# A residual stream parked in HBM during the expert stages, and its SBUF space given to two experts

## The reference, cut to what matters

```python
for layer in range(2):
    x = x + mixer[layer](rmsnorm(x, norm_mix[layer]))
    x = x + hier_moe(rmsnorm(x, norm_ffn[layer]))     # both groups share the weights
y = rmsnorm(x, norm_final)

def hier_moe(t):                       # t: (576, 1024)
    combine = ...                      # (576, 32): two nonzero weights per row
    g = einsum('td,edf->tef', t, w_gate)          # w_gate, w_up: (32, 1024, 128)
    u = einsum('td,edf->tef', t, w_up)
    hid = silu(g) * u * combine[..., None]
    return einsum('tef,efd->td', hid, w_down)     # w_down: (32, 128, 1024)
```

## Time and profile before

| | |
|---|---|
| median of three runs | 926.05 us |
| the profiled execution's own time | 925.76 us |
| its span, first to last instruction | 923.8 us |
| TensorE matmuls busy | 768.5 us, 83% |
| VectorE busy | 405.7 us, 44% |
| ScalarE busy | 259.9 us, 28% |
| GpSimd busy | 151.3 us, 16% |
| mean granted TensorE clock | 0.916 |
| DMA moved | 201.81 MB, mean 218 GB/s |
| of it on SP's queue, q1 | 161.77 MB |
| scatters and gathers, q0 | 19.75 MB |
| ScalarE's queue, q10 | 19.46 MB |

### The profile page before, as it was taken

The page is one execution under the profiler, slowest core; times in us unless marked ns, Lnnn a source line. Parts: engine busy times, 40 slices in busy tenths (PEclk is TensorE's granted clock), DMA queues, the critical chain, the costliest instruction groups (busy, mean ns, idle before and its releaser), DMA issues.

```text
span 923.8 us, 12813 instructions
## 1 busy us (share of the span) xinstructions
PE 768.5 (83%) x4895; PEld 481.0 (52%) x4895; DVE 405.7 (44%) x1001; ACT 259.9 (28%) x554; POOL 151.3 (16%) x233
## 2 busy tenths in 40 slices
PE   3899977999899898999733689799999888999730
PEld 2344445868545695555423567544345487555410
DVE  3378695867588370111128677301112162211118
ACT  6020034635111202322213355310014311322113
POOL 1020003000779001332110201000000001333110
PEclk9999996979999889999976899899999979999885
DMA  9462135000532898999869787780131296999946
GB/s 341 145 201 101 51 112 221 2 0 2 200 117 114 290 411 303 409 411 402 351 201 309 198 209 174 212 313 0 49 133 46 70 396 245 405 409 408 396 156 226
DMA packets 75381, 201.81 MB, mean 218 GB/s; under 512 B 14872, under 2 KB 29592, under 8 KB 74264
## 3 DMA queue, kind: packets, MB, share of 16 engines
q1 hardware_dynamic: 58360, 161.77, 48.7%
q0 software_dynamic: 9696, 19.75, 6.1%
q10 hardware_dynamic: 7264, 19.46, 5.8%
HBM read 171.64 MB, written 39.39 MB: 228 GB/s over the span
## 4 chain that ended last, share of the span: by engine, by line
PE 63%; DMA 11%; DVE 11%; ACT 6%; SPq 5%; issue 3%; POOL 0%; PEldq 0%; DVEq 0%; POOLq 0%; PEld 0%; ACTq 0%
PE PSUM L2049 14%; PE PSUM L1852 10%; PE PSUM L1637 8%; PE PSUM L1796 7%; PE PSUM L1873 5%; DMA RING<-in_moe_w_up 3%; PE PSUM L1840 3%; DMA RING<-in_attn_w_qkv 3%; DVE X L1515 2%; SPq L476 2%; PE PSUM L1727 2%; PE PSUM L1999 2%; PE PSUM L1995 2%; DVE XNT L773 2%; PE PSUM L1594 2%
## 5 line engine op out<-in xcount | busy, mean ns | idle before, releaser
L1637 PE MATMUL PSUM<-RING,XNT 128*128 128x512 f32 (+2 forms) x256 | 94.5, 567 | 4.3 <-DMA RING<-in_attn_w_qkv 3.6
L1852 PE MATMUL PSUM<-PH 128*64 128x256 f32 x448 | 85.6, 399 | 8.4 <-DMA PH<-in_moe_w_up 3.9
L671 POOL DMA_INDIRECT PH<-xn_scratch,PH x32 | 32.5, 1017 | 342.4 <-DVEq L1459 247.7
L2049 PE MATMUL PSUM<-PH,XNT 128*128 128x512 f32 (+1 forms) x220 | 88.1, 593 | 0.3 <-PE PSUM L2049 0.3
L1852 PE MATMUL PSUM<-RING,PH 128*64 128x256 f32 x384 | 69.4, 392 | 11.2 <-DMA PH<-in_moe_w_up 6.4
L1594 PE MATMUL PSUM<-ONES,IDENT 128*128 128x128 f32 x348 | 49.8, 314 | 24.1 <-DVEq L1518 23.9
L1490 DVE TENSOR_TENSOR PH<-PH,PSUM 128x128 f32<-128x128 f32 x32 | 9.2, 289 | 136.3 <-ACT PH L976 136.3
L1637 PEld LDWEIGHTS PSUM<-RING,XNT 128*128 128x128 f32 (+1 forms) x256 | 40.4, 177 | 53.9 <-issue 47.7
L1852 PEld LDWEIGHTS PSUM<-PH 128*64 128x64 f32 x448 | 51.6, 144 | 27.0 <-issue 11.9
L1796 PE MATMUL PSUM<-RING,PH 128*128 128x512 f32 (+1 forms) x160 | 62.6, 593 | 0.0
L1594 PEld LDWEIGHTS PSUM<-ONES,IDENT 128*128 128x128 f32 x348 | 48.8, 229 | 24.5 <-DVEq L1518 24.0
(11 more groups left out here) (378 smaller groups left out, 1366.7 us busy)
## 6 DMA issues: line engine op xcount, KB each, us to landing
PH<-in_moe_w_gate SPq DMA_DIRECT2D x28, 512.0 KB, 10.9
PH<-in_moe_w_up SPq DMA_DIRECT2D x28, 512.0 KB, 13.2
RING<-in_moe_w_gate SPq DMA_DIRECT2D x24, 512.0 KB, 11.5
RING<-in_moe_w_up SPq DMA_DIRECT2D x24, 512.0 KB, 16.0
RING<-in_moe_w_down SPq DMA_DIRECT2D x24, 512.0 KB, 16.3
PH<-in_moe_w_down SPq DMA_DIRECT2D x24, 512.0 KB, 14.8
RING<-in_attn_w_qkv SPq DMA_DIRECT2D x4, 1536.0 KB, 18.3
XNT<-in_moe_w_gate SPq DMA_DIRECT2D x12, 512.0 KB, 16.6
```

The lines of the kernel that those rows point to most:

```text
L671: pool.indirect_dma_start(out=XG[:, i % 2, :], out_offset=None, in_=xn_d[layer], in_offset=bass.IndirectOffsetOnAxis(ap=IDX[:, i:i + 1], a ...
L1637: last = te.matmul(PSUM[lo:hi, b0 + col // 512, col % 512:col % 512 + n], XT[:, c, t * P:t * P + r], RING[:, c // 2, (c % 2) * QKV + col:( ...
L1852: last = te.matmul(PSUM[m * 64:(m + 1) * 64, 2 + i % 2, 0:2 * FF], XGT[:, i % 2, c, m * 64:(m + 1) * 64], gu[:, :, c, :], start=(c == 0), ...
L2049: last = te.matmul(PSUM[p0:p0 + r, 2 * (i % 2) + w, :], XT[:, c, t * P:t * P + r], slot(SLOT[q])[:, (2 * (c % 3) + w) * 512:(2 * (c % 3) + ...
```

## The change

`X` is stored to a new HBM tensor, `residual_scratch`, tile by tile, just ahead of the store of the normed tile and on the same queue. The waits for the stores count both, 32 for a tile instead of 16. From then on two more experts use its space: expert 12 of each layer has its three matrices there, expert 13 its gate and up matrices, while its down matrix lies in `GAM`. These two places (`PARKED`) are used once in a layer. After them the twelve slots go round as before (`ring`), so each later expert stands two places later in that round. The two parked experts share one semaphore, and a wait for either waits for both. `DF` goes from 6 to 7. `residual_back` reads `X` back into place behind the last load of the layer, and the combine waits for a tile's rows and its part of `X`.

The norm's weights are now read in the middle of the stage (after pair 8's work on ScalarE), since `GAM` holds a down matrix until pair 6 is done. The read of the S5 inputs waits for pair 14 instead of pair 13, because another expert is the last in its place. At the end of the S5 layer two semaphores are merged into others (`h_transposed` into `st_transposed`, `h_copied` into `hs_in`), and `ring_wait` of TensorE takes the semaphore from the new function `filled`; these lines are not shown.

```diff
@@ -125,16 +125,24 @@
 
         xn_d = [nc.dram_tensor("xn_scratch", (NTOK, D), FP).ap()] * 2
         y_d = [nc.dram_tensor("y_scratch", (2 * NTOK, D), FP).ap()] * 2
+        x_d = nc.dram_tensor("residual_scratch", (NTOK, D), FP).ap()
         blk_d = nc.dram_tensor("block_scratch", (NB, P, BLK_F), FP).ap()
         in_d = nc.dram_tensor("input_scratch", (P, IN_F), FP).ap()
         XBASE = PH_F - XS * RW
         ZER = PH[:, PH_F - D:PH_F]
 
+        XFLAT = X.rearrange("p t d -> p (t d)")
+        PARKED = RS + XS + NS + 1
+
         def gate_up_part(k):
+            if k >= PARKED:
+                return XFLAT[:, (k - PARKED) * 2 * D:(k - PARKED + 1) * 2 * D]
             return ODD_GU if k == RS + XS + NS else slot(k)[:, 0:2 * D]
 
         def down_parts(k):
 
+            if k >= PARKED:
+                return [XFLAT[:, 4 * D:5 * D] if k == PARKED else GAM[:, :]]
             if k == RS + XS + NS:
                 return [PH[:, odd_at:odd_at + 512], MRC]
             return [slot(k)[:, 2 * D:3 * D]]
@@ -341,16 +349,29 @@
 
         Q_M = [Q_M0, Q_M1]
         ORDER0, ORDER1 = [3, 4, 5, 6, 7, 0, 1, 2, 10, 8, 9, 11], [1, 2, 3, 4, 5, 7, 6, 0, 10, 8, 9, 11]
-        SLOT = ([0, 1, 2, 3] + [0, 1, 2] + [ORDER0[e % len(ORDER0)] for e in range(NE)] 
+
+        def ring(order):
+
+            n = len(order)
+            return [order[e] if e < n else PARKED + e - n if e < n + 2 else order[(e - 2) % n] for e in range(NE)]
+
+        SLOT = ([0, 1, 2, 3] + [0, 1, 2] + ring(ORDER0) 
                 + [3, 4, 5, 7, 3, 4, 5, 7] + [3, 4, 5, 7, 6, 0]
-                + [ORDER1[e % len(ORDER1)] for e in range(NE)])
+                + ring(ORDER1))
         OV_SLOTS = [0, 1]
 
         def full(q):
 
+            if SLOT[q] >= PARKED:
+                last = q + PARKED + 1 - SLOT[q]
+                return 16 * sum(LOADS[j] for j in range(last + 1) if SLOT[j] >= PARKED)
             return 16 * sum(LOADS[j] for j in range(q + 1) if SLOT[j] == SLOT[q])
 
-        DF = 6
+        def filled(q):
+
+            return S(f"ring_full{min(SLOT[q], PARKED)}")
+
+        DF = 7
 
         def down_full(layer, i):
 
@@ -468,28 +489,35 @@
                         if e == RS + XS:
                             sp.wait_ge(S("logits"), layer + 1)
                         if e == RS + XS + 1:
-                            sp.wait_ge(S("xn_stored"), 16 * NT * (layer + 1))
+                            sp.wait_ge(S("xn_stored"), 32 * NT * (layer + 1))
                         if freed(q):
                             room(q, 0)
                         r = gate_up_part(SLOT[q])
                         for w, src in enumerate((w_gate, w_up)):
                             sp.dma_start(r[:, w * D:(w + 1) * D].rearrange("p (c f) -> p c f", c=KC),
-                                         src[layer, e].rearrange("(p c) f -> p c f", p=P)).then_inc(S(f"ring_full{SLOT[q]}"), 16)
+                                         src[layer, e].rearrange("(p c) f -> p c f", p=P)).then_inc(filled(q), 16)
                     for e in (2 * i - 2, 2 * i - 1) if i else ():
                         q = Q_M[layer] + e
                         if freed(q):
                             room(q, 1)
                         parts = down_parts(SLOT[q])
+                        if SLOT[q] > PARKED:
+                            sp.wait_ge(S("xn_done"), NT * (2 + 2 * layer))
                         if len(parts) > 1:
                             sp.wait_ge(S("routed"), layer + 1)
                         n = D // len(parts)
                         for j, dst in enumerate(parts):
                             sp.dma_start(dst, w_down[layer, e, :, j * n:(j + 1) * n]).then_inc(S(f"down_full{(i - 1) % DF}"), 16)
 
+            def residual_back(layer):
+                sp.wait_ge(S("expert_out"), PAIRS * layer + 7)
+                for t in range(NT):
+                    sp.dma_start(X[0:ROWS[t], t, :], x_d[t * P:t * P + ROWS[t], :]).then_inc(S(f"yg_full{t}"), 16)
+
             def overflow(layer):
 
                 sp.wait_ge(S("routed"), layer + 1)
-                sp.wait_ge(S("xn_stored"), 16 * NT * (layer + 1))
+                sp.wait_ge(S("xn_stored"), 32 * NT * (layer + 1))
                 sp.wait_ge(S("overflow_known"), layer + 1)
                 n = sp.value_load(OVR[0:1, layer, 0:1], min_val=0, max_val=OVP)
                 before = sp.value_load(OVR[0:1, 0, 0:1], min_val=0, max_val=OVP) if layer else 0
@@ -522,7 +550,8 @@
                 ring_load(Q_SSM + k, [(slot(SLOT[Q_SSM + k])[:, 0:BLK_F], blk_d[k])])
 
             experts(0)
-            sp.wait_ge(S("ring_free"), Q_M0 + 28)
+            residual_back(0)
+            sp.wait_ge(S("ring_free"), Q_M0 + 30)
             sp.dma_start(INS, in_d).then_inc(S("ins_in"), 16)
             sp.wait_ge(S("ring_free"), Q_M0 + 32)
             for r, src in enumerate((st_re, st_im)):
@@ -560,6 +589,7 @@
                                    src[0, 3 * j * P:(3 * j + k) * P, n * 512:(n + 1) * 512].rearrange(
                                        "(k p) n -> p k n", p=P)) for w, src in enumerate((w_ga, w_gb))])
             experts(1)
+            residual_back(1)
             overflow(1)
             rows_back(1)
 
@@ -662,7 +692,7 @@
 
             def moe(layer, ph):
                 pool.wait_ge(S("routed"), layer + 1)
-                pool.wait_ge(S("xn_stored"), 16 * NT * (layer + 1))
+                pool.wait_ge(S("xn_stored"), 32 * NT * (layer + 1))
                 n0 = PAIRS * layer
 
                 def gather(i):
@@ -800,6 +830,7 @@
         def xt_and_store(act, layer, t):
 
             xt_act(act, 1 + 2 * layer, t)
+            act.dma_start(x_d[t * P:t * P + ROWS[t], :], X[0:ROWS[t], t, :]).then_inc(S("xn_stored"), 16)
             act.dma_start(xn_d[layer][t * P:t * P + ROWS[t], :], XN[0:ROWS[t], t, :]
                           ).then_inc(S("xn_stored"), 16)
 
@@ -955,7 +986,6 @@
             end_phase(act, 3)
 
             def moe(layer, ph):
-                gamma_load(act, 2 + 2 * layer)
                 act.wait_ge(S("shifted"), 2 * layer + 1)
                 nc.scalar.activation(GE, GE, ACT.Exp).then_inc(S("exps"), 1)
                 act.wait_ge(S("shifted"), 2 * layer + 2)
@@ -989,6 +1019,8 @@
                         tokens_out(i + 1)
                     if i:
                         expert_rows(i - 1)
+                    if i == 8:
+                        gamma_load(act, 2 + 2 * layer)
                 expert_rows(PAIRS - 1)
                 act.wait_ge(S("overflow_known"), layer + 1)
                 n = act.value_load(OVR[0:1, layer, 0:1], min_val=0, max_val=OVP)
@@ -1510,7 +1542,7 @@
                 for j, t in enumerate(tiles(norm)):
                     r = ROWS[t]
 
-                    dve.wait_ge(S(f"yg_full{t}"), 16 * (layer + 1))
+                    dve.wait_ge(S(f"yg_full{t}"), 32 * (layer + 1))
                     for k in range(2):
                         ve.scalar_tensor_tensor(out=X[0:r, t, :], in0=YG[t][0:r, k, :], scalar=CW[0:r, t, k:k + 1],
                                                 in1=X[0:r, t, :], op0=ALU.mult, op1=ALU.add).then_inc(S("yg_used"), 1)
```

More of the change, by code:

```diff
@@ L1066, in _ @@
                     ins.then_inc(S("zt_ready"), 1)
-            act.wait_ge(S("h_transposed"), 1)
-            nc.scalar.activation(SOUTS, PSUM[:, 4, :].rearrange("p (k n) -> p k n", k=4), ACT.Copy).then_inc(S("h_copied"), 1)
-            nc.scalar.activation(SOUT, PSUM[0:32, 5, 0:2 * P].rearrange("p (r n) -> p r n", r=2), ACT.Copy).then_inc(S("h_copied"), 1)
-            act.wait_ge(S("h_copied"), 2)
+            act.wait_ge(S("st_transposed"), 2)
+            nc.scalar.activation(SOUTS, PSUM[:, 4, :].rearrange("p (k n) -> p k n", k=4), ACT.Copy).then_inc(S("hs_in"), 1)
+            nc.scalar.activation(SOUT, PSUM[0:32, 5, 0:2 * P].rearrange("p (r n) -> p r n", r=2), ACT.Copy).then_inc(S("hs_in"), 1)
+            act.wait_ge(S("hs_in"), 3)
             for r, (dp, ds) in enumerate(((hr_p, hr_s), (hi_p, hi_s))):
@@ L1596, in ring_wait @@
             def ring_wait(q):
-                pe.wait_ge(S(f"ring_full{SLOT[q]}"), full(q))
+                pe.wait_ge(filled(q), full(q))
             for t in range(NT):
@@ L2031, in _ @@
                         last = te.transpose(PSUM[0:32, 5, r * P:(r + 1) * P], HF[:, r, :], IDENT[:, :])
-                    last.then_inc(S("h_transposed"), 1)
+                    last.then_inc(S("st_transposed"), 1)
                 if k >= 3:
```

## The result

The change made the kernel slower. The median is 934.88 us against 927.77 us of the kernel before in the same series (17 runs of each); the ratio is 1.0064, with a 95% interval of 1.0039 to 1.0088. The ratios in this document are of runs in the faster of two states, so this one leaves out two runs of the changed kernel, of 939.95 and 2897.16 us, that the medians contain. A second series of the changed kernel gave 1.0038 (1.0000 to 1.0077). The profiled execution took 929.57 us, 3.8 us more than the one of before, and its span is 927.8 us. The forecast was 923 us, 3 us faster than before.

A forecast was written before the change was run, and what follows sets the result against it. Late weight loads, behind idle DMA gaps, were taken to bound the expert stages. Gap -8.6, stores +4.55 and tail +1.2 summed to -2.85 us, from 925.76 to 922.9, forecast 923 us; its own range 920 to 925, overall 916 to 930.

The forecast's parts named there:

- What bounded the kernel: Both expert stages: start on TensorE's time, end on the loads' time, with 19.9 us of stall to give back.
- The prediction's last part: Signs: gaps gone, last products sooner by 1 us (layer 0) and 3.5 (layer 1); if wrong, scatters landing after over 3.5.
- The gap, -8.6: Idle DMA in both layers' load stretches, filled by two more experts' loads: -8.6 us, between 6.9 and 12.5.
- The stores, +4.55: X's stores falling into the weights' prefetch push later loads back: 2.6 us in layer 0, 1.95 in layer 1.
- (b): Rival: the stores eat the gain, all of layer 0's in the way, 7.8 us with layer 1's; 926.2 us; chance 0.15.
- (e): Rival: each store holds the engines 3.2 us, not 1.3, so stores cost 11.2 us; 929.6 us; chance 0.02.
- From there on every load stands one pair earlier in the queue: Loads after the parked experts: the prefetch lasts past the release, to 360.7 in layer 0 and about 779 in layer 1.
- The tail: Stage ends: X's read back and the later S5 read slow the last scatters by 1.2 us; bounds 0 and 7.5.
- (c): Rival: read back still runs when both layers' last scatters go out, landing as in full traffic, +7.5 us; 929.2; chance 0.15.
- -4.05 in the prediction: Loads of both layers: the gap's -8.6 us together with the stores' +4.55.

The follow-up runs named there:

- e2: Changed kernel with neither store nor read back of X; X is lost and layer 1's overflow pass runs, so its total of 979.17 us says nothing.
- e11: Changed kernel with X's tiles stored once updated, layer 1's parked loads waiting for the first gather, S5 states read before X; ratio 0.9972 to before.
- e10: Kernel before plus the stores of X alone, without parked experts or read back; ratio 1.0014 to before.
- e4: Changed kernel without the stores of X, the read back taking the normed rows instead; ratio 0.9986 to before.
- e1: Kernel before plus X's stores and read back, without parked experts, S5 inputs read at the old point; ratio 1.0078 to before.
- e3: Changed kernel without the read back of X, stores kept; X is lost and layer 1's overflow pass runs, so its total of 977.59 us says nothing.
- e0: The changed kernel profiled and timed again in a second series, nothing altered; ratio 1.0038 to before.

## Why the prediction was wrong, point by point

**What bounded the kernel: right.** The stages ended on the loads, and the last products came sooner when the gaps were filled. The prediction's last part asked for 1 us in layer 0 and 3.5 in layer 1 against the stage's first; they came 3.0 and 3.65 us sooner. That layer 1 comes so close is luck: its first products were late by 2.7 us, and from the first gather on the changed kernel gains only 0.9 there (113.1 against 114.0).

**The gap, -8.6: right in size where the loads are out of the gather's way.** e2 has 4.3 us less in layer 0 and e11, from the gather on, 5.0 in layer 1: 9.3 us, between the 6.9 of the empty microseconds and the 12.5 of the mean share. No one kernel shows both: e2 itself, whose loads run beside the gather, has 2.8 us less in layer 1.

**The stores, +4.55: too much.** e10 has 0.3 us more in layer 0 and 1.1 in layer 1 than before; the changed kernel and its repeat have 1.3 to 2.3 more than e2 in layer 0, and 1.1 more than e4 from gather to last products in layer 1. Some 1.5 to 3.5 us together. The stages leave no room for the prices of rivals (b) and (e), 7.8 and 11.2 us; but e4's timed difference, 0.5 to 0.8% or some 5 to 7 us, is larger than its stages show, so (b)'s price in the changed kernel is not excluded.

**"From there on every load stands one pair earlier in the queue", so that the prefetch lasts past layer 1's release "at 768 + 7.7 = 775.7, plus the first gathers and the stores below, about 779, when loads issued at 778.16 begin to run": failed.** I moved the loads into the gap and left the release where it was. But the release follows from the first gather, and the gather used that gap: before, it landed 4.2 us after its issue; among the added loads it took 7.69, though its bytes were the same. TensorE had nothing for 2.49 us, its granted clock then fell to a half, its products took 6.44 us instead of 3.67, and SP issued its next load at 786.72. The prefetch had drained by 784. The sum had no term for this; it is the 2.7 us, and in e11, where the loads wait, they are gone. In layer 0 the gather stood in full traffic before as well (7.01 us then, 6.96 now), so nothing changed there.

**The tail, "+1.2 us": the step that decides.** It measured 5.05 + 1.9 = 6.9 us, and the timed difference between e1 and e10, some 6, agrees. Nearly all of the 1.2 was the later S5 read, at half of its 2 us (e2 and e3 put it at 0.7 to 2); the read back itself was put at next to nothing. The prediction let it run from the landing of the last up-projection at the full rate of all engines: "it starts when the last up-projection lands, 462.1, and ends at 468". In the changed kernel that load landed at 459.02, but the transfers of X had these times to landing (layer 0, then layer 1):

```profile
DMA to landing us min/median/max: 17.4/17.9/18.4
...
DMA to landing us min/median/max: 17.6/18.7/19.0
```

The last of them was issued at 454.8 and 878.8, so it landed after 472.2 and 896.4, some 13 us after the last up-projection (459.02 and 883.08) and not 6. The last scatters went out at 469.01 and 893.74. That is rival (c) with its point, the read back still running then, and it is the sign that the prediction's last part named: the loads end sooner, the rows are read no sooner (477.31 instead of 475.92 in layer 0), and the last scatters land later than 3.5 us after their issue.

In layer 0 the scatter lands as in full traffic, as (c) had it: 7.99 us, and 8.08 in e0. The landing has grown by 4.5 us, and the other half microsecond of the tail is the rows (6.16 us instead of 5.62). In layer 1, (c)'s price of 3.9 us is not borne out. The landing grew by 1.3, and the scatter goes out 0.7 us later after the last products. In e0 layer 1's tail is as long, but its scatter landed in 3.40 us, and the last products took 5.37 us instead of 3.69, with a granted clock of 0.57 over 888 to 892. So what makes layer 1's tail 1.9 us longer is not settled. That (c)'s 929.2 comes within 0.4 us of the profiled 929.57 is luck in part: it took the gain of the loads 2.6 us too small, and lacked the 2.7 us of the gather and the 1.1 of the S5 layer.

The prediction had the fact that should have led there, the unevenness of the engines, and used it to cut the gain of the gap, not to lengthen the read back, which ends on the latest engine as every load does. How uneven it is can be seen in layer 1 of the changed kernel, which has no S5 reads. From 890 to 892 only SP's queue moved bytes, with four of the five tiles of X still to land, and at a share of 0.26 that is four engines of sixteen:

```profile
890.00:891.00 1.00, 0.77 (x4) 0.40 (x6) 0.52 (x1) 0.43 (x1) 0.00 (x0) 1.00 0.26 107
891.00:892.00 1.00, 1.00 (x6) 0.17 (x2) 0.00 (x0) 0.00 (x0) 0.64 (x1) 1.00 0.26 107
```

In layer 0 the same goes on while everything waits for the scatter (windows of one microsecond). X has landed by 472.6; what runs after that is the scatter itself and the S5 reads, which stood behind X in SP's queue:

```profile
472.00:473.00 1.00, 0.00 (x0) 0.00 (x0) 0.00 (x0) 0.00 (x0) 0.00 (x0) 0.50 0.50 173
473.00:474.00 1.00, 0.00 (x0) 0.00 (x0) 0.00 (x0) 0.00 (x0) 0.00 (x0) 0.50 0.19 74
474.00:475.00 1.00, 0.00 (x0) 0.00 (x0) 0.00 (x0) 0.00 (x0) 0.00 (x0) 0.50 0.08 33
475.00:476.00 1.00, 0.00 (x0) 0.00 (x0) 0.00 (x0) 0.00 (x0) 0.00 (x0) 0.50 0.07 28
476.00:477.00 1.00, 0.00 (x0) 0.00 (x0) 0.00 (x0) 0.00 (x0) 0.00 (x0) 0.50 0.06 20
```

A share of 0.06 is as much as one engine of sixteen. The Trainium skill's page "DMA: Bandwidth & Descriptors" (Why a DMA increments its semaphore by 16 and not by 1) has the rule for this: the engines that carry a transfer finish independently, and it counts as landed with the last of them. The trace agrees: the scatter lands at 477.00, after these last microseconds at 0.06 to 0.08.

**With the terms as measured** the ledger of the loads is -6.65 us against -4.05 in the prediction, better than thought, and 6.9 and 2.7 us stand against it where the prediction had 1.2 and nothing. With the 1.1 us of the S5 layer that is the ledger's 4.0.

## What to carry to other kernels

Idle DMA time in the middle of a load-bound stage is worth filling only if nothing that the next release depends on uses it: look which short transfer, a gather here, runs in the gap, and price its landing in full traffic. Bytes that are added at the end of a stage count until the last of the sixteen engines has them, about twice the time that the mean rate gives here. Short transfers that end the stage can wait with them, as they did in layer 0. Moving them behind these is no way out when the next stage begins with reads of its own.

## What the runs showed of the hardware that was not expected

The same indirect transfer of 128 rows took 4.2 and 4.3 us to land in the gap of the loads (before, e11) and 7.69 among queued loads. After 5.71 us of small filler products, 2.49 us without work and a few transposes, TensorE's granted clock fell: it was 1.00 in each microsecond from 775 to 779, 0.76 over 778 to 780 and 0.51 over 780 to 786, so nearly all of that stretch at the lower level of 1.2 GHz. In the kernel before, with no such pause, it was 1.00, the level of 2.4 GHz, over 774 to 778. The first lines are the changed kernel's timeline of TensorE (in brackets the idle time before and what ended it), the last its window:

```profile
769.73 5.71 PE L1626 MATMUL PSUM<-ONES,IDENT 128*128 128x128 f32 x39
777.93 1.14 PE L1872 MATMUL PSUM<-IDENT,PH 128*128 128x128 f32 x8 [2.49 <-DMA PH<-xn_scratch,PH]
```

```profile
780.00:786.00 6.00, 5.76 (x28) 3.37 (x30) 0.00 (x0) 1.47 (x2) 0.83 (x1) 0.51 0.36 126
```

The first pair's 32 products took 6.44 us instead of 3.67, 2.8 us more, about as much as the late gather itself had cost. e11, without the pause, has 3.68 again.
